# A last mixer's fourth projection tile, issued in two halves around a norm's spread

## The chip, the cores and the metric

The kernel runs on one NeuronCore of a Trainium2 chip. The metric is the device time of one execution in microseconds (us). Three executions of the kernel before gave 1536.25, 1536.9 and 1539.3 us, so its median is 1536.9 us. Engines are named as in the profile: PE is TensorE's matrix multiplication and PEld its weight loads, DVE is VectorE, ACT is ScalarE, POOL is GpSimd, SP issues the transfers of the weights.

## The reference, cut to what matters

Three layers work on one sequence of 512 tokens of width 1024: an even mixer with an MLP, an odd mixer with an MLP, and a last mixer with a gated output. The place of this change is where the second block ends and the third begins:

```python
    x = x + sq_relu_mlp(rmsnorm(x, norm_mlp[layer]), w_mlp1[layer], w_mlp2[layer])
    return rmsnorm(x, final_norm)
...
        xn = _rmsnorm(h, norm_mix[i])
        u = xn @ w_in[i]
```

Two norms follow each other (`final_norm` on the output of the first block, `norm_mix` on its result), and the wide projection `w_in` follows them. Its columns are cut in three families of attention (convolution, compressed and windowed attention, dilated attention), whose softmaxes run one after another behind it.

## The kernel before, in words

**Tiles.** Everything is held transposed: 128 features on the partitions, 512 tokens along the row. A weight tile of the last projection is a block of 128x1024 that makes one output tile of 128x512, in eight products (one for each of eight input tiles). Each product is three matmuls of 128x512 (L644 to L646): weights and operands are split in a high and a low part, and high times high, high times low and low times high are added up in a PSUM bank. So an output tile is 24 matmuls, and half a tile is 12.

**Weights.** SP brings a block into a ring of four raw buffers (L614), ACT copies it to its high part (L1185), POOL subtracts that from the raw block to give the low part (L627) and signals `lo_made`. The block of the fourth projection tile (the name 11) is made ahead of the norm's root: `prepare(SUB0["zin"] // SUBS + HEAD)` at L1491.

**The double norm.** PE's `head("zin", "mix2", "final", after_down=True)` (L1008) makes the first three projection tiles (names 27, 21 and 24) in banks 4, 5 and 6, product by product as the operands of the norm come from DVE, and then the sums of squares (`norm_sums`, L702). The projections are made of unnormed operands: the factor of each token is multiplied in when DVE takes a tile out of its bank. Between the sums and that factor lies a chain: ACT root (L1203), DVE reciprocal and two small products (L1606, L2002, L2003), ACT root (L1495), DVE reciprocal and product (L1608, L1609). Then PE's `norm_spread("mix2")` (L713) spreads the factor over 128 partitions into bank 1, DVE copies it to `rms` (L1615) and multiplies the three tiles out of their banks (`evict`, L2048). Then the first scores (L749) can be made.

**The attention loop.** `attention("last", beside_last, fill_last)` runs 51 steps. In step s PE does what `beside_last` gives (in step 1 the spread of the other norm, L713 again), the scores of pair s, the values of pair s-3, the turned shares of pair s-1 (L783), and then `fill_last` draws `pace(step)` pieces of `z_fill`, the written order of the remaining projection tiles: 12 pieces in step 0. A piece is a product or a piece `part` of the compression. An aside (`Z_ASIDES`) is small work for PE that goes with a tile's product without being counted; `turn27` turns tile 27 in four 128x128 transposes (L1015). DVE in each step takes the reductions of the scores (L1709), the shares, and then `evict` for what PE finished in the step (`Z_DONE`). Tile 11 is followed on DVE by `code_positions` (L2018).

**Banks.** Projection tiles from the fourth on and asides use banks 6 and 7 in turn; `z_banks` names the bank and the tile that must have left it. PE waits for `z_ready` of that tile:

```python
            for n in range(HEAD, len(Z_HOSTS)):
                own, other = 6 + (n + 1) % 2, 6 + n % 2
                out[Z_HOSTS[n]] = (own, held.get(own))
```

The output projection behind the attention (`out2`) begins in banks 6 and 7 too, in step 44.

Of the kernel before, what the change touches and what calls it, by code (L numbers as in the profile page):

```python
# [33 lines left out]
KT = D // P  # L34
# [39 lines left out]
           10, 6, 7, 2, 4, 3, 5, 0, 1]  # L74
assert sorted(Z_HOSTS) == list(range(33))

Z_ASIDES = {3: ((4, "turn27"),), 7: ((4, "turn28"),), 10: ((4, "turn29"),), 11: ((4, "hid0"),), 14: ((4, "hid1"),),
            15: ((4, "turn14"),), 16: ((1, "gates"), (5, "cmp")), 17: ((4, "turn16"),),
            19: ((4, "lse0"),), 20: ((4, "lse1"),), 21: ((4, "lse2"),)}

# [4 lines left out]
def z_work(first=0):  # L85

    for n in range(first, len(Z_HOSTS)):
        for k in range(KT):
            for at, aside in Z_ASIDES.get(n, ()):
                if at == k:  # L90
                    yield "aside", n, aside
            yield "product", n, k
        if n in Z_PARTS:
            yield "part", n, Z_PARTS[n]
# [227 lines left out]
def pace(step):  # L322

    if step < DILATED // 2:
        return (12, 10, 10)[step // 4]
    return 4 if step < 36 else 3
# [28 lines left out]
def program(nc, x_t, stream, params, consts, ropes, p_t, out_t):  # L355
    with ExitStack() as ctx:
# [147 lines left out]
        def z_tile(name):  # L504

            return TILE0["zin"] + Z_ORDER.index(name)

        def z_banks():

            t0, held, out = TILE0["zin"], {}, {}  # L510
            for n in range(HEAD):
                out[Z_HOSTS[n]] = (4 + (t0 + n) % 4, None)
                held[4 + (t0 + n) % 4] = z_tile(Z_HOSTS[n])
            for n in range(HEAD, len(Z_HOSTS)):
                own, other = 6 + (n + 1) % 2, 6 + n % 2
                out[Z_HOSTS[n]] = (own, held.get(own))
                held[own] = z_tile(Z_HOSTS[n])
                for _, aside in Z_ASIDES.get(n, ()):
                    out[aside] = (other, held.get(other))
                    held[other] = z_tile(aside)  # L520
            return out, held
# [110 lines left out]
        def _(pe):  # L632
# [15 lines left out]
            def head(stage, op, norm, after_down=False):  # L648

                t0, b0 = TILE0[stage], SUB0[stage] // SUBS  # L650
                for k in range(KT):
                    need_split(op, k)
                    for i in range(HEAD):
                        if k == 0:
                            if t0 + i >= 4:

                                pe.wait_ge(z_ready, t0 + i - (7 if after_down else 3))
                            pe.wait_ge(lo_made, b0 + i + 1)
                        mm = product(bank[4 + (t0 + i) % 4][:, :], (b0 + i) % RING, k, *splits[op, k], k == 0, k == KT - 1)
                        if k == KT - 1:  # L660
                            mm.then_inc(acc_full, 1)
                if after_down:
                    pe.wait_ge(z_ready, t0)
                if stage == "ein":
                    pe.wait_ge(con_in, 16)
                norm_sums(norm)
# [40 lines left out]
            def norm_spread(name):  # L707

                pe.wait_ge(rtok_ready, NORM[name] + 1)
                if name == "final":  # L710
                    pe.wait_ge(rms_ready, RMS_ORDER[name])
                for t in range(TT):
                    mm = pe.matmul(bank[3 if name == "ckv" else 1][:, P * t:P * (t + 1)], rtok[:, NORM[name], t:t + 1].broadcast_to([P, P]), ident,  # L713
                                   start=True, stop=True)
                mm.then_inc(rms_full, 1)
# [290 lines left out]


            head("zin", "mix2", "final", after_down=True)  # L1008
            norm_spread("mix2")
            def turn(name):  # L1010

                host = int(name[4:])
# [96 lines left out]
            def z_fill():  # L1109

                for kind, n, what in z_work(HEAD):
                    if kind == "aside":
                        aside(what)
                        continue
                    if kind == "part":
                        part(n, *what)
                    else:
                        host, b = Z_HOSTS[n], SUB0["zin"] // SUBS + Z_BLOCK[n]
                        if what == 0:
                            if Z_BANK[host][1] is not None:  # L1120
                                pe.wait_ge(z_ready, Z_BANK[host][1] + 1)
                            pe.wait_ge(lo_made, b + 1)
                        need_split("mix2", what)
                        mm = product(bank[Z_BANK[host][0]][:, :], b % RING, what, *splits["mix2", what], what == 0, what == KT - 1)
                        if what == KT - 1:
                            mm.then_inc(acc_full, 1)
                    yield
                for i, k in OUT2_HEAD:
                    out2_part(i, k, k == 2, False)
                    yield  # L1130

            filling = z_fill()

            def fill_last(step):
                for _ in range(pace(step)):
                    next(filling, None)

            def beside_last(step):
# [1215 lines left out]
```

## Time and profile before

| | |
|---|---|
| median of three executions | 1536.9 us |
| profiled execution, own time | 1539.17 us |
| profiled execution, span from first to last instruction | 1537.3 us |
| mean granted clock of TensorE over the span | 0.981 |
| PE busy | 1463.7 us, 95% |
| DVE, ACT, POOL busy | 789.1, 605.2, 569.0 us |
| moved from and to HBM | 126.58 MB read, 2.10 MB written |

The own time of an execution lies 1.87 us above its span. PE is busy nearly all the time, so time is won where it stands idle, where its clock is low, or by less work. A line number in the profile is that of the kernel before. A granted clock of 1.00 is 2.4 GHz, one of 0.50 is 1.2 GHz.

### The profile page before, as it was taken

To read this page: it belongs to the slowest core of one execution; us is meant where nothing else is said; L and a number is where in the kernel's file an instruction comes from. 1 tells how busy PE (TensorE), PEld (TensorE's weight loads), DVE (VectorE), ACT (ScalarE), POOL (GpSimd) and SP (SyncE) were. 2 spreads that over 40 slices of the span, in tenths; PEclk is the share of its full clock that TensorE was granted. 3 is DMA by queue.
4 is the path that set the end of the run, shared out by engine and by line. 5 is a ranking of instruction groups with operands and counts; after the bars stand their busy time and mean duration, and the time that the engine had idled before them with its cause. 6 is when DMAs were issued, how large, how long until landed. Compare 5 with 4: busy or idle time off the path is not lost.

```text
span 1537.3 us, 20393 instructions
## 1 busy us (share of the span) xinstructions
PE 1463.7 (95%) x7122; PEld 1147.1 (75%) x7122; DVE 789.1 (51%) x1413; ACT 605.2 (39%) x1104; POOL 569.0 (37%) x236
## 2 busy tenths in 40 slices
PE   6988999999999999789999999999989999999996
PEld 5656878888888887446778888888868777766785
DVE  6875542223444578894452223444467337675434
ACT  5343432232222436764432223222254335554432
POOL 3222354444444344211344444444434642222340
PEclk9999999999999999899999999999999999999998
DMA  5111222222222222100222222222222321111111
GB/s 214 66 55 56 97 96 96 96 96 96 97 98 99 88 96 69 55 29 28 69 96 96 96 96 96 98 98 100 98 73 96 133 88 65 45 56 55 69 69 55
DMA packets 36624, 129.55 MB, mean 84 GB/s; under 512 B 4048, under 2 KB 4176, under 8 KB 36560
## 3 DMA queue, kind: packets, MB, share of 16 engines
q1 hardware_dynamic: 35136, 124.80, 23.3%
q10 hardware_dynamic: 1424, 3.90, 0.7%
q8 instruction: 40, 0.66, 0.2%
q14 instruction: 24, 0.20, 0.0%
HBM read 126.58 MB, written 2.10 MB: 84 GB/s over the span
## 4 chain that ended last, share of the span: by engine, by line
PE 45%; issue 37%; POOL 14%; DVE 3%; ACT 1%; POOLq 0%; DVEq 0%; ACTq 0%
POOL w L627 14%; PE bank L644 13%; PE bank L646 13%; PE bank L645 13%; PE bank L769 2%; PE bank L783 2%; PE bank L749 1%; PE bank L1080 0%; DVE rms L1631 0%; DVE arena L2048 0%; PE bank L713 0%; DVE opC L1599 0%; DVE arena L2169 0%; PE bank L702 0%; DVE arena L1782 0%
## 5 line engine op out<-in xcount | busy, mean ns | idle before, releaser
L627 POOL TENSOR_TENSOR w<-raw,w 128x1024 fp32r<-128x1024 f32 x232 | 568.8, 2455 | 934.4 <-ACT w L1185 555.6
L644 PE MATMUL bank<-opC,w 128*128 128x512 f32 x624 | 254.7, 408 | 15.2 <-DVE opC L1599 10.7
L646 PE MATMUL bank<-opC,w 128*128 128x512 f32 x624 | 246.2, 395 | 0.0
L645 PE MATMUL bank<-opC,w 128*128 128x512 f32 x624 | 246.2, 395 | 0.0
L1758 DVE TENSOR_TENSOR mlp_op<-arena,mlp_op 128x512 fp32r<-128x512 f32 x64 | 144.5, 2260 | 188.7 <-ACT mlp_op L1300 188.7
L1272 ACT ACTIVATE w<-raw 128x1024 fp32r<-128x1024 f32 x126 | 133.2, 1057 | 239.5 <-PE bank L646 239.5
L644 PE MATMUL bank<-mlp_op,w 128*128 128x512 f32 x544 | 212.2, 390 | 3.1 <-ACT arena L1390 1.4
L646 PE MATMUL bank<-mlp_op,w 128*128 128x512 f32 x544 | 211.7, 389 | 0.0
L645 PE MATMUL bank<-mlp_op,w 128*128 128x512 f32 x544 | 211.7, 389 | 0.0
L644 PE MATMUL bank<-opA,w 128*128 128x512 f32 x416 | 162.7, 391 | 2.3 <-DVE arena L1753 1.4
L646 PE MATMUL bank<-opA,w 128*128 128x512 f32 x416 | 161.9, 389 | 0.0
L645 PE MATMUL bank<-opA,w 128*128 128x512 f32 x416 | 161.9, 389 | 0.0
L1751 DVE TENSOR_TENSOR tmp<-tmp,rms 128x512 f32<-128x512 f32 x64 | 51.5, 804 | 211.0 <-ACT tmp L1280 210.5
L644 PEld LDWEIGHTS bank<-opC,w 128*128 128x128 f32 x624 | 118.9, 191 | 43.8 <-DVE opC L1599 11.9
L646 PEld LDWEIGHTS bank<-opC,w 128*128 128x128 f32 x624 | 119.0, 191 | 26.3
L645 PEld LDWEIGHTS bank<-opC,w 128*128 128x128 f32 x624 | 119.3, 191 | 23.1 <-issue 0.5
L1280 ACT ACTIVATE tmp<-bank 128x512 f32<-128x512 f32 x64 | 38.3, 598 | 224.5 <-PE bank L646 213.8
L1185 ACT ACTIVATE w<-raw 128x1024 fp32r<-128x1024 f32 x106 | 110.1, 1051 | 37.4 <-PE bank L646 36.6
L644 PEld LDWEIGHTS bank<-mlp_op,w 128*128 128x128 f32 x544 | 102.1, 188 | 26.0 <-ACT arena L1390 2.3
L646 PEld LDWEIGHTS bank<-mlp_op,w 128*128 128x128 f32 x544 | 102.1, 188 | 21.4
L645 PEld LDWEIGHTS bank<-mlp_op,w 128*128 128x128 f32 x544 | 102.1, 188 | 20.9
L749 PE MATMUL bank<-arena 64*128 64x512 f32 (+4 forms) x336 | 77.2, 544 | 17.3 <-DVE arena L1686 8.3
(218 smaller groups left out, 1930.3 us busy)
## 6 DMA issues: line engine op xcount, KB each, us to landing
raw<-stream_dram SPq DMA_DIRECT2D x232, 512.0 KB, 3.4
out_t_dram<-arena SPq DMA_DIRECT2D x8, 256.0 KB, 2.1
x<-x_t_dram SPq DMA_DIRECT2D x4, 256.0 KB, 5.8
x<-x_t_dram ACTq DMA_DIRECT2D x4, 256.0 KB, 6.9
rope<-ropes_dram ACTq DMA_DIRECT2D x2, 512.0 KB, 6.8
con<-consts_dram ACTq DMA_DIRECT2D x1, 993.5 KB, 8.1
arena<-p_t_dram ACTq DMA_DIRECT2D x1, 512.0 KB, 3.6
par<-params_dram ACTq DMA_DIRECT2D x1, 253.5 KB, 4.1
```

The costliest lines, as they stand in the source:

```text
L627: pool.tensor_tensor(w_lo[:, j, :], raw[:, j, :], w_hi[:, j, :].bitcast(F32), ALU.subtract).then_inc(lo_made, 1)
L644: pe.matmul(out, wh, hi, start=first, stop=False)
L645: pe.matmul(out, wh, lo, start=False, stop=False)
L646: return pe.matmul(out, wl, hi, start=False, stop=last)
L749: mm = pe.matmul(bank[2 + i % 2][:, 0:u["n"]], *u["qk"][part], start=part == 0, stop=part == parts - 1)
L769: mm = pe.matmul(into[at:at + 64, col:col + P], u["v"][b], tmp[0:kw, 4 + half, P * b:P * (b + 1)], start=(b == 0 and u.get("first", True)) ...
L783: mm = pe.transpose(bank[4 + i % 2][0:w, a:a + P], probs(i, SEQ)[:, a:a + w], ident)
L1185: nc.scalar.activation(w_hi[:, b % RING, :], raw[:, b % RING, :], ACT.Copy).then_inc(hi_made, 1)
L1272: nc.scalar.activation(w_hi[:, b % RING, :], raw[:, b % RING, :], ACT.Copy).then_inc(hi_made, 1)
L1280: nc.scalar.activation(tmp[:, j % 2, :], bank[4 + (t0 + j) % 4][:, :], ACT.Relu).then_inc(relu_made, 1)
L1751: TTn(tmp[:, j % 2, :], tmp[:, j % 2, :], rms[:, 1, :], ALU.mult).then_inc(vstep, 1)
L1758: TTn(mlp_op[:, 1, j % 2, :], u[:, bass.ds(SEQ * RING * i + SEQ * j, SEQ)], mlp_op[:, 0, j % 2, :].bitcast(F32), ALU.subtract).then_inc(ml ...
```

## The change

The spread of `mix2` leaves its place behind the head. `z_fill` is started at once; its first eight pieces are the eight products of tile 11. Four are issued ahead of the spread and four behind it, and step 0 of the attention draws eight pieces fewer. The aside `turn27` moves from tile 11's fifth product to tile 12's second. Banks 6 and 7 change places for every tile and aside of the loop, so that tile 11 goes into bank 7, which no tile of the head holds, instead of bank 6, which tile 24 holds.

```diff
-Z_ASIDES = {3: ((4, "turn27"),), 7: ((4, "turn28"),), 10: ((4, "turn29"),), 11: ((4, "hid0"),), 14: ((4, "hid1"),),
+Z_ASIDES = {4: ((1, "turn27"),), 7: ((4, "turn28"),), 10: ((4, "turn29"),), 11: ((4, "hid0"),), 14: ((4, "hid1"),),
...
             for n in range(HEAD, len(Z_HOSTS)):
-                own, other = 6 + (n + 1) % 2, 6 + n % 2
+                own, other = 6 + n % 2, 6 + (n + 1) % 2
...
             head("zin", "mix2", "final", after_down=True)
-            norm_spread("mix2")
             def turn(name):
...
             filling = z_fill()
+            for k in range(KT):
+                if k == KT // 2:
+                    norm_spread("mix2")
+                next(filling)
 
             def fill_last(step):
-                for _ in range(pace(step)):
+                for _ in range(pace(step) - (KT if step == 0 else 0)):
                     next(filling, None)
```

**Order on PE, around the spread.** Before, PE goes from the sums to the spread, to the scores of pair 0 and to tile 11, in bank 6:

```order
L702 MATMUL bank0<-con,rms 128x1 x7
L713 MATMUL bank1<-con,rtok 128x128 [waits rtok_ready]
L713 MATMUL bank1<-con,rtok 128x128 x3
L749 MATMUL bank2<-arena 128x128 [waits z_ready]
L749 MATMUL bank3<-arena 128x128
L644 MATMUL bank6<-opC_51,w 128x512 [waits lo_made,z_ready]
L645 MATMUL bank6<-opC_51,w 128x512
```

Now tile 11, in bank 7, begins behind the sums (its twelve matmuls are cut to the first and last here), and its wait names `lo_made` alone:

```order
L702 MATMUL bank0<-con,rms 128x1 x7
L644 MATMUL bank7<-opC_51,w 128x512 [waits lo_made]
...
L646 MATMUL bank7<-opC_51,w 128x512
L713 MATMUL bank1<-con,rtok 128x128 [waits rtok_ready]
L713 MATMUL bank1<-con,rtok 128x128 x3
L644 MATMUL bank7<-opC_51,w 128x512
```

The spread stands twelve matmuls later in PE's order, and twelve more stand between it and the scores.

**Order on PE, behind the scores of pair 0, with the turn of tile 27.** Before, twelve matmuls of tile 11 stand between the scores and the turn. Now it is three of tile 12, and the turn's bank is the one that tile 11 has just filled (its `z_ready` is now that of tile 11):

```order
L749 MATMUL bank3<-arena 128x128
L644 MATMUL bank6<-opC_51,w 128x512 [waits lo_made,z_ready]
L645 MATMUL bank6<-opC_51,w 128x512
L646 MATMUL bank6<-opC_51,w 128x512
L1014 MATMUL bank7<-con,arena 128x128 [waits z_ready]
L1014 MATMUL bank7<-con,arena 128x128 x3
```

L1014 is L1015 of the kernel before. The turn has come nearer to the scores, by nine matmuls.

**Order on DVE, in step 0 behind the reductions of pair 0.** Before:

```order
L1709 ISA negm 128x1
L2043 COPY arena<-bank7 128x512 [waits acc_full]
L2048 TENSOR_TENSOR arena<-bank6,rms 128x512 [waits acc_full]
L2018 TENSOR_TENSOR arena<-arena,par 128x512 [waits z_ready]
L2017 MEMSET arena 128x16
```

Now (line numbers of DVE's part are three higher):

```order
L1712 ISA negm 128x1
L2051 TENSOR_TENSOR arena<-bank7,rms 128x512 [waits acc_full]
L2021 TENSOR_TENSOR arena<-arena,par 128x512 [waits z_ready]
L2020 MEMSET arena 128x16
L2021 TENSOR_TENSOR arena<-arena,par 128x496 [waits vstep]
L2046 COPY arena<-bank7 128x512 [waits acc_full]
```

Tile 11 leaves its bank first, and the turned tile 27 is copied behind the coding of tile 11. The orders on ACT, POOL and SP are as before.

## Rows read from the trace of the kernel before

**Rows 1.** Page: busy time of PE and of the other engines.

```profile
PE 1463.7 (95%) x7122; PEld 1147.1 (75%) x7122; DVE 789.1 (51%) x1413; ACT 605.2 (39%) x1104; POOL 569.0 (37%) x236
```

**Rows 2.** Windows: busy us by engine (PE, PEld, DVE, ACT, POOL), then granted clock.

```profile
1138.92:1140.61 1.69, 0.00 (x0) 0.00 (x0) 0.84 (x5) 1.02 (x3) 0.00 (x0) 1.00 0.53 189
1141.78:1144.47 2.69, 0.00 (x0) 0.00 (x0) 2.58 (x4) 2.50 (x3) 2.69 (x2) 0.50 0.00 0
1145.21:1149.62 4.41, 4.41 (x14) 3.48 (x13) 0.51 (x4) 0.88 (x4) 2.97 (x2) 0.62 0.66 225
...
1216.69:1220.11 3.42, 3.42 (x11) 2.68 (x10) 0.31 (x2) 3.10 (x8) 0.95 (x1) 0.52 0.26 99
```

**Rows 3.** Timeline, PE: start, length, line, operation, count, idle time before it.

```profile
1137.08 1.84 PE L702 MATMUL bank<-con,rms 128*128 128x1 f32 x16
...
1140.62 1.16 PE L713 MATMUL bank<-con,rtok 128*128 128x128 f32 x8 [1.70 <-DVE rtok L1609]
...
1144.48 0.80 PE L749 MATMUL bank<-arena 64*128 64x128 f32 x4 [2.70 <-DVE arena L2048]
...
1155.54 1.05 PE L713 MATMUL bank<-con,rtok 128*128 128x128 f32 x8
1156.53 0.70 PE L749 MATMUL bank<-arena 64*128 64x256 f32 x4
```

**Rows 4.** Timeline, DVE between the sums and the scores.

```profile
1140.40 0.16 DVE L1609 TENSOR_TENSOR rtok<-small,rtok 128x4 f32<-128x4 f32 x1
1141.81 0.69 DVE L1615 COPY rms<-bank 128x512 f32<-128x512 f32 x1 [1.25 <-PE bank L713]
1142.54 1.89 DVE L2048 TENSOR_TENSOR arena<-bank,rms 128x512 f32<-128x512 f32 x3
```

**Rows 5.** Timeline, ACT and POOL: the weight blocks around the norm.

```profile
1134.85 1.04 ACT L1185 ACTIVATE w<-raw 128x1024 fp32r<-128x1024 f32 x1
...
1135.97 2.49 POOL L627 TENSOR_TENSOR w<-raw,w 128x1024 fp32r<-128x1024 f32 x1 [18.37 <-ACT w L1185]
...
1141.18 7.00 POOL L627 TENSOR_TENSOR w<-raw,w 128x1024 fp32r<-128x1024 f32 x3 [2.71 <-ACT w L1185]
```

**Rows 6.** Timeline, PE: first and last of 22 matmuls at full clock.

```profile
1150.54 0.40 PE L646 MATMUL bank<-opC,w 128*128 128x512 f32 x1
...
1155.32 0.39 PE L646 MATMUL bank<-opC,w 128*128 128x512 f32 x1
```

**Rows 7.** Timeline, near 1385 us: scores of 128 columns (PE), end of reductions (DVE).

```profile
1384.43 0.49 PE L749 MATMUL bank<-arena 64*128 64x128 f32 x4
1384.85 1.09 PE L769 MATMUL bank<-tmp,arena 128*64 128x128 f32 x16
...
1385.49 0.08 DVE L1709 DVE_READ_ACCUMULATOR2_ANT negm<- 128x1 f32 x1
```

**Rows 8.** Timeline, near 1150 us: the turn (PE), tile 11's eviction and coding (DVE).

```profile
1149.63 0.60 PE L1015 MATMUL bank<-con,arena 128*128 128x128 f32 x4
...
1153.02 0.69 DVE L2048 TENSOR_TENSOR arena<-bank,rms 128x512 f32<-128x512 f32 x1 [2.06 <-PE bank L646]
1153.75 0.69 DVE L2018 TENSOR_TENSOR arena<-arena,par 128x512 f32<-128x512 f32 x1
```

**Rows 9.** Timeline: DVE's L2062 alone and beside POOL, PE behind DVE.

```profile
1160.89 0.74 DVE L2062 SCALAR_TENSOR_TENSOR x<-x,par,rms 128x512 f32<-128x512 f32 x1
...
1207.69 7.14 POOL L627 TENSOR_TENSOR w<-raw,w 128x1024 fp32r<-128x1024 f32 x3 [4.70 <-ACT w L1185]
...
1212.97 2.41 DVE L2062 SCALAR_TENSOR_TENSOR x<-x,par,rms 128x512 f32<-128x512 f32 x1
...
1216.13 0.44 PE L769 MATMUL bank<-tmp,arena 128*64 128x128 f32 x4 [2.45 <-DVE arena L2112]
```

**Rows 10.** Timeline, near 1408 us: last projection tile leaves (DVE), output projection begins (PE).

```profile
1407.44 0.69 DVE L2048 TENSOR_TENSOR arena<-bank,rms 128x512 f32<-128x512 f32 x1 [1.42 <-PE bank L646]
...
1408.93 0.48 PE L644 MATMUL bank<-op_any,w 128*128 128x512 f32 x1
```

## The prediction, made before the changed kernel ran

> **What bounds the kernel now.** I read the page first: PE is busy 95% of the span [rows 1], so an edit pays only where PE stands idle or where its clock is low. Then the windows around the double norm [rows 2]. Between the end of the sums (1137.08 + 1.84 = 1138.92) and the spread PE does nothing for 1.69 us, and between the spread and the first scores nothing for another 2.69 us, the second time at a granted clock of 0.50. The first window after the scores has a clock of 0.62: PE fell to 1.2 GHz after these gaps and came back to 2.4 GHz only some 3 us into the next products. PE's timeline gives the four marks [rows 3]: sums end 1138.92, spread 1140.62, scores 1144.48, and step 1 (the other norm's spread) 1155.54. From 1138.92 to 1155.54 are 16.62 us, and this is the stretch that the change rewrites. The releasers stand in the same rows: the spread waits for DVE's last small product, the scores for DVE's third eviction. DVE's rows [rows 4] show what lies between: the factor is there at 1140.56, the copy of the spread starts 0.03 us after the spread's end (1141.78) and three evictions end at 1144.43.
>
> Behind step 0 I expect a rigid shift, because the steps there are set by what PE issues, and ACT, DVE, POOL and SP follow PE's signals.
>
> **The change, part by part.** Full-clock price of a matmul: 21 intervals from 1150.54 to 1155.32 are 4.78 us, 0.2276 us each [rows 6]. Half a tile (12) is 2.73 us.
>
> *The half ahead.* It needs three things. Its operands are those that the head has just used. Its bank, 7, is held by no head tile; down's tile left it before the sums, and the order shows only `lo_made` at the wait. Its weights: ACT made the high part at 1134.85, POOL the low part from 1135.97 to 1138.46 [rows 5], 0.46 us before the sums end. So it runs from 1138.92 to 1141.65. Of its 2.73 us, 1.7 fill the wait for the factor, and the spread, which could start at 1140.6, comes 1.04 us late.
>
> *The spread* takes 1.05 us at full clock (1.16 before) [rows 3]: until 1142.70. DVE's copy and three evictions then take 2.62 us (1141.81 to 1144.43) [rows 4], with 0.03 ahead: until 1145.35. Scores at 1145.40, 0.92 later than before.
>
> *The half behind* takes 2.73 us from about 1142.64 (PE issues it as the spread's last part drains, as the scores follow 0.99 us after the start of a spread [rows 3]) to 1145.37. Its cover is DVE's 2.62 us, and the two end together. A few hundredths either way cost as much. Tile 11 is complete when the scores start.
>
> *Step 0.* Scores of 128 columns to the next instruction: 0.42 us at full clock [rows 7]; before it was 0.73 (1144.48 to 1145.21). Three matmuls of tile 12 take 0.68 us, to 1146.50. Then comes a **new wait**: the turn writes bank 7, and DVE must take tile 11 out first. DVE is through the reductions 1.14 us after the scores' start (1384.43 to 1385.57 [rows 7]), and an eviction takes 0.69 us and 0.04 between the two [rows 8]: 1145.40 + 1.14 + 0.73 = 1147.27. PE goes on at 1147.32, so it stands for 0.82 us. Behind it on PE are the turn, nine matmuls and step 1. The turn (0.60 us of records, of which the next product overlaps a part [rows 8]) I price at 0.44, what the chain gave it, then nine matmuls, 2.05: step 0 ends at 1149.81, where it ended at 1155.54.
>
> The gain is 5.73 us. As a ledger: idle time filled 1.69 + 2.69 = 4.38; clock given back 0.31 on the scores, 0.11 on the spread and 1.68 on the first twelve matmuls (4.41 us in the window [rows 2] instead of 2.73), together 2.10; less the new wait 0.82. That is 5.66, and 0.07 of rounding and issue.
>
> *The turn's copy* now stands on DVE behind the coding of tile 11 (two additions with 0.69 each [rows 8]): ready at about 1149.5. Bank 7 is next written by tile 28, whose matmuls begin 1 + 0.6 + 2.7 us into step 1, near 1154.1. The margin is over 4 us: nothing. DVE is also needed at 1151.4 for the next reductions, 1.9 us later: nothing. ACT's block for tile 12 and the two after it are made at 1141.18 to 1148.18 as before [rows 5]; tile 12 needs the first of them, ready near 1143.5, at 1145.8: nothing. SP issues as before.
>
> *The swap of banks* moves one late wait: the output projection's first tile, in step 44, now shares its bank with the very last projection tile instead of the last but one. DVE took that tile out from 1407.44 to 1408.13, and the output projection began at 1408.93 [rows 10]: a margin of 0.8 us in a part whose order does not change. Nothing.
>
> **A figure of the Trainium skill.** The rows say 0.2276 us for a matmul of 512 columns with its weights changing each time. The Trainium skill, "TensorE: Matmul & The Clock Gate", section "Back-to-back issue gap", gives about 131 ns as the sustained spacing in a stream of loads and matmuls of 512 columns. By that the half ahead would take 1.6 us, would end before the factor is there and would not delay the spread; but 24 matmuls taken out of step 0 would be 3.1 us instead of 5.46, so the sum, as an estimate from that page, would be some 2.3 us smaller, near 3.4. The trace disagrees with it by a factor of 1.7 for this kernel's operands, and I go by the trace.
>
> **The sum.** The profiled execution took 1539.17 us itself, so it would take 1533.5. It lies 2.3 us above the median of the three shown (1536.9), which I take as the place to start from: 1536.9 - 5.7 = 1531.2. The gap between profile and median has the size of one low-clock stretch: the one near 1217 us, 3.42 us at clock 0.52 [rows 2], costs 3.42 x 0.48 = 1.6 us. The clock's part of my gain (2.10) may be smaller in other executions, so the bounds of the gain are 3.6 us (no clock given back) and 7.3 (one such stretch less behind it), 1533.3 and 1529.6 us.
>
> **The rivals.** *DVE is held up by POOL at the turn.* POOL subtracts from 1141.18 to 1148.18 [rows 5]. Near 1213 us an operation of DVE took 2.41 us beside POOL instead of 0.74, PE stood 2.45 us behind it [rows 9], and the low clock followed. If tile 11's eviction is held until POOL ends at 1148.18, it ends 1.6 us later, PE's new wait becomes 2.4 us and the gain 4.1: 1532.8. Against it: the three evictions ran beside POOL at 1.89 / 3 = 0.63 us each [rows 4, 5]. Chance 0.07. The Trainium skill, "SBUF — State Buffer", section "Who interferes with whom", says that a DVE instruction with two SBUF inputs contends with POOL's reads and one with at most one does not. By that rule the eviction (bank and `rms`) is free and only tile 11's coding, now beside POOL, is held, by 0.9 us at its start, which the 1.9 us above cover.
>
> *The gain is given back behind step 0.* The later idle places of PE (2.45 us near 1214 [rows 9], for one) are followed by low clock. If the shift makes two more such stretches of 1.6 us, or lengthens the ones there, 2.5 us are left: 1534.4. For it: the executions already differ by 3 us. Against: nothing in those steps changes its order. Chance 0.11.
>
> *Slower: the low part comes late.* PE now stands at `lo_made` with the spread queued behind it, and DVE's evictions, the scores and every later step behind that. Lateness there is not hidden any more. Up to 0.46 us is free; it eats the gain from 6.2 us on, a low part after 1144.6. If the wait were met only by the last of the three later blocks (1148.18), PE would start 9.3 us late, the time would be 1536.9 - 5.7 + 9.3 = 1540.5. Against it: the block is the one converted ahead of the root. Chance 0.02.
>
> *It does not do what it says*, tile 11 waiting for a head tile's bank: the order of the changed program has no such wait, so it has no chance of its own.
>
> **Chances and range.** The forecast, a gain near 5.7, has 0.80. The range holds it with its bounds and the first two rivals, with 0.7 us more below, by which the lowest of the three executions shown lies under their median: 1528.9 to 1534.6 us. A measurement of this kernel can tell 0.2%, 3.1 us, from no change: faster means below 1533.8. That takes in the forecast, the first rival and a fifth of the second: 0.89. Within 0.2%: 0.09. Slower: 0.02.
>
> **What would show it.** Twelve matmuls between sums and spread, none with an idle time above 0.1 us; the spread 2.7 us after the sums; scores 6.5 us after them (5.6 before); a wait of about 0.8 us ahead of the turn, released by DVE's eviction; clock 1.00 through the whole stretch; step 1's spread 10.9 us after the sums instead of 16.6; the same distances from there to the end. Wrong would be: a granted clock of 0.50 in step 0, a wait for POOL ahead of tile 11, a longer distance from step 1 to the end, or a wait at the start of the output projection.

## The result, and the profile after

The changed kernel took 1526.18 to 1528.92 us in four executions, median 1527.62, against 1537.95 for the kernel before (four executions). The ratio is 0.9935, with a 95% interval of 0.9923 to 0.9947: 10.3 us less, clearly faster by the bound of 0.2%. The forecast was 1531.2 with a range from 1528.9 to 1534.6, so the time lies below the range. The forecast started from 1536.9, the median of three executions of the kernel before; with the fourth it is 1537.95. The profiled execution took 1526.18 us, its span is 1524.4 us, its mean granted clock 0.989 (0.981 before).

The page of the changed kernel, answering to [rows 1]: the same instructions, PE 8.7 us less busy.

```profile
span 1524.4 us, 20393 instructions
PE 1455.0 (95%) x7122; PEld 1140.8 (75%) x7122; DVE 790.8 (52%) x1413; ACT 605.0 (40%) x1104; POOL 569.4 (37%) x236
```

Two windows cut the rest of the span at the prediction's marks, the end of the sums and the start of step 1 (columns as in [rows 2]). Of the changed kernel:

```profile
1135.90:1146.64 10.74, 10.45 (x52) 8.14 (x53) 7.09 (x18) 6.27 (x12) 7.09 (x3) 1.00 0.51 153
1146.64:1524.40 377.76, 356.34 (x1947) 273.25 (x1945) 208.27 (x554) 161.10 (x398) 127.77 (x52) 0.98 0.23 76
```

Of the kernel before:

```profile
1138.92:1155.54 16.62, 12.22 (x52) 9.91 (x53) 6.71 (x18) 6.54 (x12) 7.00 (x3) 0.79 0.37 127
1155.54:1537.30 381.76, 360.45 (x1947) 276.49 (x1945) 207.04 (x553) 160.97 (x398) 127.72 (x52) 0.97 0.21 74
```

The stretch that the change rewrites went from 16.62 to 10.74 us, at a granted clock of 1.00 instead of 0.79. Behind it 4.00 us more have gone. The remaining 3.0 us of the 12.9 between the two spans lie ahead of the sums (1138.92 against 1135.90), where both programs are the same. That part is chance: in the 18 traces of this case the sums end between 1135.8 and 1144.9 us, on average at 1138.9 in the eight with the order of before around the norm and at 1139.1 in the ten with the changed one, and it goes with the clock (27.3 us at 1.2 GHz ahead of the sums in the trace of before, 20.5 in the changed kernel's).

PE's timeline of the changed kernel, answering to [rows 3] and [rows 8]:

```profile
1134.06 1.84 PE L702 MATMUL bank<-con,rms 128*128 128x1 f32 x16
...
1135.76 0.49 PE L644 MATMUL bank<-opC,w 128*128 128x512 f32 x1
...
1138.62 1.05 PE L713 MATMUL bank<-con,rtok 128*128 128x128 f32 x8
...
1142.38 0.49 PE L749 MATMUL bank<-arena 64*128 64x128 f32 x4
1142.80 0.51 PE L644 MATMUL bank<-opC,w 128*128 128x512 f32 x1
...
1144.07 0.66 PE L1014 MATMUL bank<-con,arena 128*128 128x128 f32 x4 [0.29 <-DVE arena L2051]
...
1146.64 1.05 PE L713 MATMUL bank<-con,rtok 128*128 128x128 f32 x8
```

The half tile starts in the sums' wake, the spread comes 2.72 us behind the sums (forecast 2.7), the scores 6.48 (forecast 6.5), and step 1 10.74 (forecast 10.9). Ahead of the turn (L1014) stands the new wait. The profile puts it at 0.29 us; from start to start it is 0.46, since after the third matmul at 1143.38 the next could have started at 1143.61. It was forecast with 0.82, from start to start.

DVE and POOL beside it, answering to [rows 4], [rows 5] and [rows 8]:

```profile
1132.88 2.49 POOL L627 TENSOR_TENSOR w<-raw,w 128x1024 fp32r<-128x1024 f32 x1 [18.36 <-ACT w L1188]
...
1138.16 7.09 POOL L627 TENSOR_TENSOR w<-raw,w 128x1024 fp32r<-128x1024 f32 x3 [2.78 <-ACT w L1188]
...
1139.71 0.69 DVE L1618 COPY rms<-bank 128x512 f32<-128x512 f32 x1 [2.17 <-PE bank L713]
...
1140.43 1.89 DVE L2051 TENSOR_TENSOR arena<-bank,rms 128x512 f32<-128x512 f32 x3
...
1143.33 0.69 DVE L2051 TENSOR_TENSOR arena<-bank,rms 128x512 f32<-128x512 f32 x1
...
1144.05 1.75 DVE L2021 TENSOR_TENSOR arena<-arena,par 128x512 f32<-128x512 f32 x1
...
1145.86 0.68 DVE L2021 TENSOR_TENSOR arena<-arena,par 128x496 f32<-128x496 f32 x1
1146.45 0.68 DVE L2046 COPY arena<-bank 128x512 f32<-128x512 f32 x1
```

The low part of tile 11's block was there at 1135.37, 0.5 us before the sums ended. The evictions beside POOL took 1.89 us for three again, and tile 11's eviction (1143.33) 0.69. Its coding (1144.05) took 1.75 us instead of the 0.69 of [rows 8]: both its inputs are in SBUF, and POOL's subtractions ran beside it until 1145.25; the second addition, behind them, took 0.68. The Trainium skill, "SBUF — State Buffer", section "Who interferes with whom", says that a DVE instruction with two SBUF inputs contends with a POOL instruction that reads SBUF. The trace agrees. As forecast nobody waited for it.

So where did the 4.00 us behind step 1 come from? PE's waits there are the same in both traces (values behind ACT 4.2 us, scores behind DVE 2.8, values behind DVE's L2112 2.7). The clock isn't. Windows of the kernel before, the three places behind step 1 where it was at 1.2 GHz:

```profile
1216.90:1220.30 3.40, 3.40 (x10) 2.66 (x9) 0.10 (x1) 3.10 (x8) 1.15 (x1) 0.50 0.19 74
1322.70:1326.10 3.40, 3.40 (x23) 3.07 (x24) 0.12 (x1) 1.18 (x2) 2.35 (x1) 0.50 0.00 0
1414.80:1418.20 3.40, 3.40 (x10) 2.22 (x10) 0.45 (x1) 0.85 (x3) 2.68 (x1) 0.50 0.00 0
```

The changed kernel near the same three places of the program, from some 9 us earlier on:

```profile
1207.00:1211.00 4.00, 3.76 (x14) 2.95 (x15) 1.11 (x9) 2.56 (x8) 0.33 (x1) 0.58 0.45 131
1311.00:1316.00 5.00, 3.11 (x32) 2.47 (x31) 2.71 (x12) 4.11 (x12) 1.43 (x1) 1.00 0.00 0
1400.00:1404.00 4.00, 2.53 (x19) 1.78 (x18) 4.00 (x19) 3.58 (x11) 0.53 (x1) 1.00 0.00 0
```

and PE at the second of them:

```profile
1311.22 0.49 PE L749 MATMUL bank<-arena 64*128 64x128 f32 x4
1313.60 1.09 PE L769 MATMUL bank<-tmp,arena 128*64 128x128 f32 x16 [1.89 <-ACT tmp L1246]
```

PE waits 1.89 us there, as it did before, yet the clock stays at 1.00. Each stretch at 1.2 GHz costs about 1.7 us, an estimate (3.40 us at a clock of 0.50). Two of three are gone, some 3.4 of the 4.0 us. The rest is in the output's tail, behind PE's last wait of 3.0 us. There the clock had fallen ahead of the last norm's sums in the kernel before, and only behind them in the changed one:

```profile
1524.79 1.86 PE L702 MATMUL bank<-con,rms 128*128 128x1 f32 x8 [3.00 <-DVE rms L1631]
```

```profile
1512.62 1.05 PE L702 MATMUL bank<-con,rms 128*128 128x1 f32 x8 [3.01 <-DVE rms L1634]
```

These sums took 0.8 us less.

### The profile page after: what moved, and what is told of

It is laid out like the page before. It is cut to its first block, busy times and chain, and to the rows that moved or that the text cites. A ratio compares the mean times of both kernels' runs of the same rounds, so it can differ in the third digit from the quotient of the medians.

```text
span 1524.4 us, 20393 instructions
## 1 busy us (share of the span) xinstructions
PE 1455.0 (95%) x7122; PEld 1140.8 (75%) x7122; DVE 790.8 (52%) x1413; ACT 605.0 (40%) x1104; POOL 569.4 (37%) x236
## 4 chain that ended last, share of the span: by engine, by line
PE 45%; issue 37%; POOL 14%; DVE 3%; ACT 1%; POOLq 0%; DVEq 0%; ACTq 0%
POOL w L627 14%; PE bank L644 13%; PE bank L646 13%; PE bank L645 13%; PE bank L769 2%; PE bank L783 2%; PE bank L749 1%; PE bank L1079 0%; DVE rms L1634 0%; DVE opC L1602 0%; PE bank L713 0%; DVE arena L2172 0%; DVE arena L2051 0%; PE bank L702 0%; DVE arena L1785 0%
## 5 line engine op out<-in xcount | busy, mean ns | idle before, releaser
L644 PE MATMUL bank<-opC,w 128*128 128x512 f32 x624 | 253.5, 406 | 15.0 <-DVE opC L1602 10.5
L644 PEld LDWEIGHTS bank<-opA,w 128*128 128x128 f32 x416 | 78.1, 188 | 19.3 <-issue 3.3
```

The costliest lines, as they stand in the source:

```text
L644: pe.matmul(out, wh, hi, start=first, stop=False)
```

## The experiments

Theories, after the result. **Chance (A):** the clock falls behind PE's idle places at random, and the four executions were lucky. **Position (B):** which idle places are followed by 1.2 GHz depends on where in time they fall, so that a shift of all that follows moves the mean. **Something else (C):** the swapped banks or the turn's new place gain by themselves.

All kernels that ran, with median and executions, the ratio to the kernel before run beside them, and from the trace: sums to step 1, step 1 to the end, and what the clock took in this last part (half the time that PE's clock was at 1.2 GHz between step 1 and the wait of 3.0 us ahead of the output's tail; the tail is left out). Ratios are the safer comparison between rows: behind the first pair, the rows come from four groups of runs, on three chips, and the kernel before had medians from 1536.7 to 1538.0 in them.

| kernel | median us | ratio, 95% interval | sums to step 1 | step 1 to end | lost to the clock there |
|---|---|---|---|---|---|
| before, first trace | 1537.95 (4) | | 16.62 | 381.76 | 5.1 |
| before again | 1536.88 (10) | 0.9997, 0.9986 to 1.0009 | 16.58 | 377.47 | 1.7 |
| change, first trace | 1527.62 (4) | 0.9935, 0.9923 to 0.9947 | 10.74 | 377.76 | 1.7 |
| change again | 1528.49 (7) | 0.9943, 0.9927 to 0.9958 | 10.75 | 377.67 | 1.7 |
| all eight behind | 1532.50 (10) | 0.9976, 0.9960 to 0.9992 | 14.13 | 380.76 | 5.1 |
| all eight ahead | 1535.32 (10) | 0.9979, 0.9968 to 0.9990 | 14.54 | 380.81 | 5.1 |
| before, gaps warm | 1533.53 (8) | 0.9974, 0.9961 to 0.9987 | 14.78 | 380.67 | 5.1 |
| change, pad of 3 | 1534.07 (10) | 0.9980, 0.9969 to 0.9991 | 12.78 | 379.53 | 3.4 |
| change, pad of 5 | 1531.75 (6) | 0.9965, 0.9952 to 0.9977 | 14.15 | 380.83 | 5.1 |
| change, pad of 8 | 1539.52 (10) | 1.0008, 0.9996 to 1.0020 | 16.20 | 382.62 | 6.8 |
| change, turn later | 1528.39 (10) | 0.9944, 0.9924 to 0.9964 | 10.22 | 377.57 | 1.7 |
| banks and turn only | 1533.47 (10) | 0.9976, 0.9967 to 0.9986 | 16.91 | 377.55 | 1.7 |
| banks only | 1537.97 (10) | 1.0006, 0.9996 to 1.0016 | 16.72 | 382.01 | 5.1 |
| before, pad of 0.3 us | 1534.96 (10) | 0.9985, 0.9974 to 0.9996 | 18.47 | 376.35 | 0 |
| before, earlier fill | 1527.72 (4) | 0.9937, 0.9920 to 0.9954 | 16.58 | 370.79 | 0 |
| banks and turn, earlier fill | 1528.16 (4) | 0.9943, 0.9926 to 0.9959 | 16.97 | 371.14 | 0 |
| change, earlier fill | 1522.06 (4) | 0.9891, 0.9874 to 0.9907 | 10.74 | 371.27 | 0 |
| the same, turn later | 1523.73 (4) | 0.9911, 0.9892 to 0.9930 | 10.23 | 372.21 | 0 |

Down to the pad of 0.3 us, the sixth column explains the fifth: it is 376 us plus what the clock took, within 0.9 us. The two that lie 0.7 and 0.9 us above (before, first trace, and banks only) are those where the low clock of the tail began 13 us before the end, instead of 9 to 11.

PE's waits behind step 1 are the same in these 14 traces, and the low clock follows the long ones: it fell within or behind the wait of 2.45 us in 13 of the 14, behind the one of 1.89 us in eight, behind the one of 1.38 in none, behind one of 0.78 and 0.67 close together in one, and behind one of 0.66 and 0.81 close together in three.

### The same two kernels again

The kernel before, with no edit:

> The kernel before, unchanged, for its spread from one execution to the next and for a second trace. Theory A (the extra gain comes from stretches of low TensorE clock that fall at random, and the profiled pair was a lucky one): its trace has low-clock stretches of 1.2 GHz at other places than the first (near 1216, 1322 and 1414 us behind the norm), and their number behind step 1 varies. Theory B (they belong to the program's timing behind the norm, so the shift of the change removes them every time): the same stretches behind step 1, counted from step 1's start, as in the first trace; the stretch from the sums to step 1 takes 16.6 us again, and from step 1 to the end 381.8 us.

```profile
1140.95:1157.53 16.58, 12.19 (x52) 9.79 (x53) 6.70 (x18) 6.53 (x12) 6.98 (x3) 0.79 0.38 127
1157.53:1535.00 377.47, 356.15 (x1947) 272.95 (x1945) 207.03 (x553) 160.84 (x398) 127.77 (x52) 0.98 0.21 74
```

The stretch is the same within 0.04 us; the rest is 4.3 us shorter than in the first trace of the same program, with one stretch of low clock instead of three. So what the profiled pair showed behind step 1 was partly chance: B in the form "the same stretches every time" is wrong. Over the ten executions the time goes with the mean granted clock, from 1533.8 us at 0.986 to 1539.5 at 0.981.

The changed kernel, with no edit:

> The changed kernel, unchanged, for more executions and a second trace. From the sums to step 1 it takes 10.7 to 10.9 us again, whatever the rest does. Theory A (the extra 4 to 5 us are chance, four lucky executions): the median of ten comes near 1531. Theory B (the position behind the norm decides which idle places of PE are followed by low clock): it stays near 1527.6, with values in steps of 1.7 to 2.5 us around it.

```profile
1138.08:1148.83 10.75, 10.44 (x54) 8.14 (x53) 7.09 (x18) 6.29 (x12) 7.08 (x3) 1.00 0.47 153
1148.83:1526.50 377.67, 356.33 (x1947) 273.13 (x1945) 208.25 (x554) 161.15 (x398) 127.84 (x52) 0.98 0.22 76
```

Stretch and rest are as in its first trace, and the median of seven stays at 1528.49, 8.4 us below the kernel before. A alone, which wanted 1531, does not hold either. The second pair of profiled executions does not show where the excess over the stretch lies: of the 8.5 us between their spans 5.8 are the stretch, 2.9 are ahead of the sums, where the programs are the same, and behind step 1 the changed kernel is 0.2 us longer. That the excess lies behind step 1 follows only for the mean: three sets of executions with the changed order (1527.62, 1528.49 and, with the turn later, 1528.39) lie 8.4 to 10.3 us below the kernel before, their stretches are shorter by 5.8 to 6.4, and ahead of the sums the order makes no difference. What is left for B: the executions vary, but their mean depends on the position.

### The two halves, and their places

```diff
             for k in range(KT):
-                if k == KT // 2:
+                if k == 0:
                     norm_spread("mix2")
                 next(filling)
```

> All eight products of tile 11 behind the spread. By the ledger of the prediction (idle time filled, DVE's evictions as the cover): the wait of 1.69 us for the factor is back, the spread 1.0 us earlier than in the change, the eight products 5.46 us long against DVE's 2.6 us, so the scores come 1.7 us later than in the change, and step 1 is 12.6 us behind the sums instead of 10.9. The time is that of the change plus 1.7 us if nothing behind step 1 changes, 1529.3 us. If the low-clock stretches behind step 1 come back with a shift of that size, up to 3.4 us more.

```profile
1143.40:1146.80 3.40, 3.40 (x12) 2.73 (x11) 2.58 (x4) 2.86 (x3) 3.40 (x2) 0.50 0.08 13
```

The stretch took 14.13 us, 1.5 more than expected, because this idle time of 1.69 us was followed by 3.4 us at 1.2 GHz. The half ahead is worth 3.4 us in the traces: 1.7 of idle time, 1.7 of clock.

All eight ahead, with the spread behind the loop:

```diff
             for k in range(KT):
-                if k == KT // 2:
-                    norm_spread("mix2")
                 next(filling)
+            norm_spread("mix2")
```

> All eight products of tile 11 ahead of the spread. The factor is there long before PE is: the spread starts 5.46 us behind the sums, and DVE's copy and evictions (2.65 us) stand uncovered behind it: the scores 2.7 us later than in the change, step 1 13.6 us behind the sums, 1530.3 us, if the clock stays at 2.4 GHz and nothing behind step 1 changes. If low-clock stretches come back behind step 1, up to 3.4 us more.

```profile
1144.49 1.05 PE L713 MATMUL bank<-con,rtok 128*128 128x128 f32 x8
1148.25 0.49 PE L749 MATMUL bank<-arena 64*128 64x128 f32 x4 [2.71 <-DVE arena L2050]
```

PE waits 2.71 us for DVE's evictions, as the prediction's cover has it, and low clock follows: 14.54 us, 0.9 more than expected. The split in halves beats both ends by the trace and by the median. The whole times lie 3.2 and 5.0 us above what was expected with nothing changed behind step 1 (1529.3 and 1530.3); 0.9 to 1.5 of that is the stretch, and both traces have 10.2 us at 1.2 GHz behind step 1, as the first trace of before.

The gaps of the kernel before filled with idle work, 7 matmuls ahead of the spread and 11 behind it, into bank 7:

```diff
+            pe.wait_ge(lo_made, SUB0["zin"] // SUBS + HEAD + 1)
+            idle(7)
             norm_spread("mix2")
+            idle(11)
```

> The kernel before with the two idle gaps around the spread filled by 7 and 11 matmuls whose result nobody reads; no work is moved. Theory of the ledger (2.1 us of the stretch's gain are clock, 4.4 us are idle time filled with useful work, the wait at the turn takes 0.3 to 0.8): the granted clock is 1.00 in step 0, the stretch from the sums to step 1 takes 16.6 - 2.1 = 14.5 us. Rival (the clock falls anyway, or the gain is all from the moved work): 16.6 us. The whole time may lie off by the low-clock stretches behind step 1.

```profile
1136.65:1151.43 14.78, 14.60 (x71) 11.51 (x71) 6.70 (x18) 6.54 (x12) 7.09 (x3) 1.00 0.41 143
```

The clock is 1.00 through the stretch, and 16.6 went to 14.78: 1.8 us, where the ledger said 2.1 for the clock. Against the change's 10.75, 4.0 us are left for the moved work, less the wait at the turn.

### Pads behind the norm

Repeated products of tile 12, whose sum nobody reads, at the end of step 0 of the changed kernel; N is 3, 5 and 8:

```diff
             def fill_last(step):
                 for _ in range(pace(step) - (KT if step == 0 else 0)):
                     next(filling, None)
+                for _ in range(N if step == 0 else 0):
+                    product(bank[0][:, :], (SUB0["zin"] // SUBS + Z_BLOCK[4]) % RING, 0, *splits["mix2", 0], True, True)
```

> The change with eight repeated products (24 matmuls into a bank that nobody reads, 5.46 us) at the end of step 0, so that all behind it stands nearly where it stood before the change, and PE has no new idle time. Theory rigid shift: plus 5.5 us, 1533.1. Theory B (the position behind the norm decides on the low-clock stretches that follow): the 4.0 us gained behind step 1 are lost again, 1537. Theory A (chance): 1533.1 in the mean, with a varying number of stretches in the traces.

```profile
1138.98:1155.18 16.20, 15.90 (x78) 12.65 (x78) 7.57 (x18) 7.79 (x13) 9.47 (x4) 1.00 0.41 135
1155.18:1537.80 382.62, 361.22 (x1947) 276.98 (x1945) 206.35 (x553) 160.01 (x396) 125.34 (x51) 0.97 0.21 73
```

> The change with three repeated products (9 matmuls, 2.05 us) at the end of step 0. Rigid shift: plus 2.0 us on the changed kernel, 1529.7. Theory B: low-clock stretches behind the norm depend on where PE's idle places fall, not on how much is saved; this pad puts them in the same relation to the clock's changes as the pad of eight, which cost 11.9 us for 5.5 us of work, so it costs far more than its 2.0 us: 1534 to 1536.

```profile
1138.59:1151.37 12.78, 12.47 (x62) 9.83 (x63) 7.57 (x18) 7.78 (x13) 7.54 (x4) 1.00 0.48 165
1151.37:1530.90 379.53, 358.17 (x1947) 274.77 (x1945) 206.22 (x553) 159.65 (x396) 127.21 (x52) 0.98 0.21 74
```

> The change with five repeated products (15 matmuls, 3.41 us) at the end of step 0. Rigid shift: plus 3.4 us, 1531.0. Theory B expects the same 1531.0 here, since by the traces' edges of the clock this pad restores the relation that the change has without a pad, and so a lower time than the smaller pad of three. A theory by which any delay behind the norm costs clock (monotonic) expects more than with three, 1536 or above.

```profile
1141.02:1155.17 14.15, 13.85 (x68) 10.95 (x69) 7.57 (x18) 7.78 (x13) 8.91 (x4) 1.00 0.43 149
1155.17:1536.00 380.83, 359.41 (x1947) 275.49 (x1945) 206.32 (x553) 159.73 (x396) 125.91 (x52) 0.97 0.21 74
```

In the stretch each pad costs just its work: 12.78, 14.15 and 16.20 are 10.75 plus 2.0, 3.4 and 5.45. The whole is another matter. By the medians a pad of 2.0 us costs 5.6 us, one of 3.4 costs 3.3, and one of 5.5 costs 11.0 (against 1528.5). A rigid shift would have given 2.0, 3.4 and 5.5. The pad of 8 is beyond it by any reading of its interval (B had 1537, a rigid shift 1533.1, and 1539.52 came), and it makes the change as slow as the kernel before. That 3 is dearer than 5 is what B said, but the two intervals overlap, so the pair only points that way. (The profiled execution of the pad of 5 is its slowest, 1537.75.)

### Banks, turn, and 0.3 us

The kernel before with swapped banks and the turn's new place, nothing else of the change:

> The kernel before with the swap of banks 6 and 7 and the new place of the turn, but tile 11 all behind the first scores, as it was. Prediction's reading (the swap costs and gains nothing, its late wait has 0.8 us of margin): the stretch from the sums to step 1 takes 16.6 us, or up to 0.5 less or more by the turn's place, no wait at the start of the output projection, 1536.9. If part of the unexplained gain came from the banks, it is 2 us or more faster.

```profile
1135.84:1152.75 16.91, 12.41 (x53) 9.80 (x53) 6.61 (x18) 7.32 (x13) 6.99 (x3) 0.80 0.40 125
1152.75:1530.30 377.55, 356.20 (x1947) 273.04 (x1945) 206.24 (x553) 160.06 (x397) 127.75 (x52) 0.98 0.22 74
```

The stretch was 0.3 us longer, within the 0.5 that was expected, and yet the kernel was faster by 3.7 us (2.2 to 5.1 by the interval). This made C a live theory. First the banks alone, with the turn where it was:

```diff
-                own, other = 6 + (n + 1) % 2, 6 + n % 2
+                own, other = 6 + n % 2, 6 + (n + 1) % 2
```

> The kernel before with banks 6 and 7 exchanged and nothing else: the turn stays ahead of tile 11's fifth product. The stretch from the sums to step 1 is 16.6 us. If the banks gain: 1533 to 1534. If only the position behind the norm counts: as the kernel before, 1536.8 to 1538.

As the kernel before (1.0006): the banks gain nothing. The turn's place alone was not run. Then the shift alone, without banks or turn:

```diff
             def fill_last(step):
                 for _ in range(pace(step)):
                     next(filling, None)
+                for n in ((512, 256) if step == 0 else ()):
+                    pe.matmul(bank[0][:, 0:n], w_hi[:, (SUB0["zin"] // SUBS + Z_BLOCK[4]) % RING, 0:P],
+                              splits["mix2", 0][0][:, 0:n], start=True, stop=True)
```

> The kernel before with two more matmuls (512 and 256 columns, some 0.34 us, into a bank that nobody reads) at the end of step 0, banks and turn as before. The stretch is 16.9 us, as with the banks and turn of the change alone. If only the position behind the norm counts, it is faster than the kernel before although it does more: 1533 to 1535. If the banks gain: 0.3 us slower than before, 1537 to 1538.

Two matmuls more, and the kernel is faster: 0.9985, interval 0.9974 to 0.9996. Its profiled execution is its slowest (1541.51 us): it came to the sums only at 1144.88, had 10.2 us of low clock on end between them and step 1, and none from there to the tail, so its trace says little of the others. C is no longer needed; a shift of 0.3 us alone moves the time by 2.3 us, 0.6 to 4.0 by the interval. That is the weakest of these comparisons, one of many, and what the banks and the turn gave beyond it (3.7 us) was not told apart from it.

### The idle places filled

If the clock falls behind PE's idle places, taking those away must take away what it costs in the part behind step 1. In five steps of the attention loop, pieces of the step's own fill are drawn earlier, into the places where PE stood; no work is added:

```diff
+            EARLY = {7: (0, 4), 25: (0, 3), 35: (2, 0), 40: (1, 1), 45: (1, 1)}
...
                     beside(step)
+                    early(step, 0)
                     if step < pairs:
                         scores(step)
+                    early(step, 1)
                     if step >= VALUE_LAG:
                         values(step - VALUE_LAG)
...
-                for _ in range(pace(step) - (KT if step == 0 else 0)):
+                for _ in range(pace(step) - sum(EARLY.get(step, (0, 0))) - (KT if step == 0 else 0)):
```

> The changed kernel with eleven later pieces of fill drawn earlier within their own step, into the places where PE waits behind step 1: in step 7 four ahead of the values, in step 25 three ahead of the values, in step 35 two ahead of the scores, in steps 40 and 45 one ahead of the scores and one ahead of the values. Those waits are 2.4, 1.9, 1.4, 1.5 and 1.5 us. Theory B (low clock comes behind these idle places, at some positions of them): with the waits gone no low-clock stretch is left between step 1 and the output projection, whatever the execution; from step 1 to the end 370 to 373 us instead of 377.7, and the whole near 1522. Rival (the low clock has another cause than these waits, or the chain of the softmax is late in any case): the waits move and the stretches stay, 1528 or more.

```profile
1138.39:1149.13 10.74, 10.43 (x52) 8.13 (x53) 7.08 (x18) 6.28 (x12) 7.08 (x3) 1.00 0.52 151
1149.13:1520.40 371.27, 355.98 (x1947) 271.82 (x1945) 211.41 (x554) 161.09 (x398) 127.71 (x52) 0.99 0.23 77
```

```profile
1206.79 0.49 PE L749 MATMUL bank<-arena 64*128 64x128 f32 x4
1207.21 0.50 PE L644 MATMUL bank<-opC,w 128*128 128x512 f32 x1
...
1210.16 0.44 PE L769 MATMUL bank<-tmp,arena 128*64 128x128 f32 x4
```

In step 7 twelve matmuls now stand between the scores and the values, where PE stood 2.45 us [rows 9] and fell to 1.2 GHz. The waits that are left behind step 1 are of 1.05 and 0.63 us. No stretch of low clock is left between step 1 and the output's tail, and the kernel takes 1522.06 us, 0.9891 of the kernel before, the lowest median of all that ran.

> The same earlier fill in the kernel before. Theory B: the part behind step 1 now costs the same in both kernels, so the change is worth what its own stretch gives: this kernel lies 5.9 us above the changed kernel with the earlier fill, not 8 to 10. Rival (the change gains behind step 1 by something else than the clock, such as banks or order): it lies 8 to 10 us above it.

```profile
1138.43:1155.01 16.58, 12.18 (x52) 9.86 (x53) 6.70 (x18) 6.54 (x12) 7.01 (x3) 0.79 0.39 127
1155.01:1525.80 370.79, 355.54 (x1947) 271.37 (x1945) 210.30 (x553) 161.03 (x398) 127.75 (x52) 0.99 0.23 76
```

By the traces this is the cleanest measure of the change: with the long waits gone, the part behind step 1 costs the same in both within 0.5 us (370.79 and 371.27), and the stretch differs by 5.84 us, where the prediction said 5.73. The two medians differ by 5.66 us, the means of the same executions by 6.7. With four executions each, spread over 3 us, the whole times alone could not tell 5.8 from 8.4.

> Swapped banks and the turn's new place in the kernel before, with the earlier fill that takes the idle places behind step 1 away. If the gain of the banks was clock behind those idle places: 0.3 us above the kernel before with the earlier fill, 1527.5 to 1529. If the banks gain by themselves: 3 us below it, near 1525.

1528.16 us, 0.4 above the kernel before with the earlier fill (by the ratios 0.9943 and 0.9937, whose intervals overlap), where a gain by themselves would have given 1525: the gain of banks and turn is gone with the idle places, the second sign against C.

### The turn's place

```diff
-Z_ASIDES = {4: ((1, "turn27"),),
+Z_ASIDES = {4: ((3, "turn27"),),
```

> The change with the turn of tile 27 ahead of tile 12's fourth product instead of its second, so that DVE has taken tile 11 out long before. The change's trace shows a wait of 0.29 us there where 0.82 was predicted. If it is the eviction alone: no wait, the stretch 10.4 to 10.5 us instead of 10.75. If PE then waits elsewhere: 10.75. The whole time by the low-clock stretches behind: 1528 give or take 2.

The wait is gone and the stretch is 10.22 us, 0.53 shorter (10.4 to 10.5 was expected). The whole (1528.39) can't be told from the change's. The same edit on top of the earlier fill:

> The changed kernel with the earlier fill in steps 7, 25, 35, 40 and 45 and the turn of tile 27 ahead of tile 12's fourth product. 0.5 us below the changed kernel with the earlier fill alone: 1521.5. No low-clock stretch behind the sums until the output's tail.

1523.73 us, where 1521.5 was expected; its stretch is 10.23, the part behind 0.9 us longer (372.21), and its profiled execution came to the sums 2.9 us later than the other's. The intervals of the two versions overlap. Whether the turn's later place helps stays open.

## Why the prediction was wrong

**What bounds the kernel, and the stretch.** Right. The idle 1.69 and 2.69 us and the clock of 0.50 were what there was to gain. The half ahead hidden for 1.7 us and delaying the spread by 1.0, the spread at 2.7 us and the scores at 6.5, the half behind as long as DVE's evictions: each as forecast within 0.03 us. The rivals of a late low part and of a held eviction did not come.

**The new wait.** Right in place and releaser, too large: 0.46 us from start to start instead of 0.82. DVE began tile 11's eviction 0.95 us behind the scores' start (1142.38 to 1143.33), where the sum had 1.18 (1.14 and a gap of 0.04), which is 0.23 us less; the other 0.13 is PE's own, since the scores and three matmuls took it 1.23 us and not 1.10. This made the gain of the stretch 5.88 in the profiled pair instead of 5.73.

**The ledger.** 5.66 us were expected from clock (2.1), idle time (4.4) and wait; warming the gaps alone measured 1.8 for the clock, and from there to the change are 4.0 us, where idle time less wait was 3.6.

**Margins at nothing.** Right: the turn's copy, the banks' late wait (swapping them alone: 1.0006), the next reductions. The copy was ready 11.2 us behind the sums instead of 10.6, since the coding ahead of it was slow, and DVE then stood idle for 1.33 us before the next reductions, where the margin had been put at 1.9.

**Behind step 0: the step that failed.** "Behind step 0 I expect a rigid shift". PE's work and waits did shift rigidly, but the clock behind those waits did not. I priced it only as a bound ("one such stretch less", 7.3 us) and gave the loss by it a chance of 0.11 and the gain none of its own. In the profiled pair the part behind step 1 was 4.0 us shorter, two stretches of low clock and 0.8 us in the tail, where the forecast had nothing. By medians the change is worth 5.7 us (means: 6.7) where the long waits behind it are filled, and 8.4 to 10.3 where they are not. The trace of before showed three stretches behind the norm, 5.1 us of clock, all behind waits of PE; with all three priced (5.7 + 5.1 us) the range would have held the result. Why the changed position draws less low clock on average stays open.

**The place to start from** was one profile and three executions. The 2.3 us between profile and median were of the size of one low-clock stretch, as said; the kernel before varies by more than twice that from one execution to the next (1533.8 to 1539.5 in ten), much of it ahead of the sums. The start was 0.2 to 1.05 us off, and the gain of 8.4 to 10.3 us does not rest on it.

## What to carry to other kernels

Fill the wait for a norm's factor with half of the next tile, and DVE's evictions behind it with the other half: the price is read from the waits' lengths and came out within 0.2 us. But where PE waits behind the edit and its clock has fallen there, an edit's time is known only to the stretches of low clock in that part, and its trace must be split into the part ahead, the part that the edit rewrites and the part behind. To measure the edit itself, fill the long waits of the rest in both kernels; that took the stretches of low clock out of the part behind and, by moved work alone, some 10 us off the kernel before and 6 off the changed one.

## What the runs showed of the hardware

- The same wait of PE is followed by low clock in one execution and not in the next: 1.89 us at step 25 gave 3.4 us at 1.2 GHz in the first trace of the kernel before and none in the second. Over 14 traces it was followed by low clock in eight, the wait of 2.45 us in 13, the one of 1.38 us in none.
- The same program reached the end of the norm's sums between 1135.8 and 1144.9 us in 18 traces, with 17 to 34 us at 1.2 GHz ahead of it.
- A shift of 0.3 us by two extra matmuls made a kernel faster (0.9985, 0.9974 to 0.9996), and a pad of 5.5 us cost 11.0 us.
- Behind step 1 the time was 376 us plus what the clock took, for every order and pad that left PE's waits in place. With the waits in five steps filled it was 370.8 to 372.2, and no trace of four showed low clock there ahead of the tail. Why the position matters was not tried further than this.
- A DVE addition with both inputs in SBUF took 1.75 us instead of 0.69 while POOL subtracted, and evictions from a bank took 0.63 each as before.
